# A mixture of experts and two hybrid layers on one core: the last two expert turns written out, the expert output spread in two parts by token tile, the first layer's norm between its adds

## The reference, cut to what matters

```python
out = jnp.zeros_like(t)
for e in range(N_EXPERTS):                       # 32 experts, D_FF_EXP = 512
    hid = jax.nn.silu(t @ w_eg[e]) * (t @ w_eu[e])
    out = out + gates[:, e:e + 1] * (hid @ w_ed[e])
...
x = x + hier_moe(h2, w_rg[l], b_rg[l], w_re[l], b_re[l], w_eg[l], w_eu[l], w_ed[l])
...                                              # first_block ends in rmsnorm(x, normf_g)
h = rms_norm(x, norm_mix)                        # hybrid_layer, DEPTH_2 = 2 times
proj = h @ w_in
```

## Time and profile before

| | |
|---|---|
| median of 3 runs | 1846.59 us |
| profiled execution | 1845.76 us |
| its span | 1844.0 us |
| PE busy | 1741.5 us, 94% of the span |
| DVE, ACT, POOL busy | 883.2, 730.7, 109.2 us |
| moved | 412.19 MB |
| experts on PE (first `pick` to last `spread`) | 181.7 to 651.7 us |

### The profile page before, as it was taken

The page is one execution under the profiler, slowest core; times in us unless marked ns, Lnnn a source line. Parts: engine busy times, 40 slices in busy tenths (PEclk is TensorE's granted clock), DMA queues, the critical chain, the costliest instruction groups (busy, mean ns, idle before and its releaser), DMA issues.

```text
span 1844.0 us, 27291 instructions
## 1 busy us (share of the span) xinstructions
PE 1741.5 (94%) x11548; PEld 1384.4 (75%) x11548; DVE 883.2 (48%) x1445; ACT 730.7 (40%) x1076; POOL 109.2 (6%) x116
## 2 busy tenths in 40 slices
PE   7996999889998889999999999999999999999998
PEld 6985344434444379888899999888988889989986
DVE  5484111111111164643468966536553447886643
ACT  4462111111111044654556444324575455644432
POOL 0000000000000001410200000000150020000000
PEclk9997999999999988999999999999999999999999
DMA  7344799999999845233334354544433233444452
GB/s 270 119 186 188 303 429 429 428 430 428 428 429 428 364 184 228 93 138 138 124 122 160 144 190 183 207 159 180 187 138 134 95 137 138 164 185 162 183 212 98
DMA packets 31304, 412.19 MB, mean 224 GB/s; under 512 B 3649, under 2 KB 5217, under 8 KB 6497
## 3 DMA queue, kind: packets, MB, share of 16 engines
q1 hardware_dynamic: 31200, 410.70, 55.9%
HBM read 408.85 MB, written 1.84 MB: 223 GB/s over the span
## 4 chain that ended last, share of the span: by engine, by line
PE 83%; DMA 9%; DVE 3%; ACT 2%; issue 2%; SPq 0%; POOL 0%; DVEq 0%; POOLq 0%; ACTq 0%
PE bank L1149 11%; PE bank L1154 11%; PE bank L1150 11%; PE bank L1064 9%; DMA work_mem<-in_w 8%; PE bank L1162 4%; PE bank L1163 4%; PE bank L1161 4%; PE bank L1081 4%; PE bank L1187 2%; PE bank L1188 2%; PE bank L1193 2%; DMA wring<-in_w 1%; PE bank L1473 1%; PE bank L1043 1%
## 5 line engine op out<-in xcount | busy, mean ns | idle before, releaser
L1789 ACT ACTIVATE w_hi<-wring 128x2048 fp32r<-128x2048 f32 x84 | 161.0, 1917 | 252.1 <-PE bank L1150 130.8
L2473 DVE TENSOR_TENSOR w_lo<-wring,w_hi 128x2048 fp32r<-128x2048 f32 x84 | 192.1, 2291 | 136.0 <-ACT w_hi L1789 135.9
L1149 PE MATMUL bank<-mixed_hi,w_hi_early 128*128 128x256 f32 x960 | 241.5, 290 | 4.9 <-DVE mixed_lo L2481 2.5
L1789 ACT ACTIVATE w_hi_early<-wring 128x2048 fp32r<-128x2048 f32 x84 | 160.7, 1913 | 203.6 <-PE bank L1150 142.6
L1150 PE MATMUL bank<-mixed_lo,w_hi_early 128*128 128x256 f32 x960 | 235.4, 283 | 0.0
L2473 DVE TENSOR_TENSOR w_lo<-wring,w_hi_early 128x2048 fp32r<-128x2048 f32 x84 | 191.6, 2285 | 75.0 <-ACT w_hi_early L1789 74.6
L1154 PE MATMUL bank<-mixed_hi,w_lo 128*128 128x256 f32 x1472 | 206.5, 283 | 0.0
L1149 PEld LDWEIGHTS bank<-mixed_hi,w_hi_early 128*128 128x128 f32 x960 | 183.7, 191 | 11.7 <-DVE w_lo L2473 4.6
L1154 PEld LDWEIGHTS bank<-mixed_hi,w_lo 128*128 128x128 f32 x1472 | 189.9, 192 | 0.0
L1150 PEld LDWEIGHTS bank<-mixed_lo,w_hi_early 128*128 128x128 f32 x960 | 184.3, 192 | 0.1
L1064 PE MATMUL bank<-wring,gates_mem 128*64 128x512 f32 x768 | 168.3, 594 | 12.3 <-DMA wring<-in_w 12.3
(11 more groups left out here) (482 smaller groups left out, 3089.0 us busy)
## 6 DMA issues: line engine op xcount, KB each, us to landing
wring<-in_w SPq DMA_DIRECT2D x160, 2048.0 KB, 8.8
work_mem<-in_w SPq DMA_DIRECT2D x32, 2048.0 KB, 17.9
cst<-in_const SPq DMA_DIRECT2D x1, 1224.0 KB, 16.3
prm<-in_prm SPq DMA_DIRECT2D x3, 381.0 KB, 8.6
x_mem<-in_x SPq DMA_DIRECT2D x2, 512.0 KB, 4.9
out_x<-x_mem SPq DMA_DIRECT2D x2, 512.0 KB, 2.6
rel_skew<-work_mem SPq DMA_DIRECT2D x1, 768.0 KB, 3.5
work_mem<-in_prm SPq DMA_DIRECT2D x1, 512.0 KB, 16.4
```

Of the source, the lines that this page charges most:

```text
L1149: pe.matmul(out, w[0][:, k, cols], x[0][:, k, :], start=(k == 0), stop=False)
L1789: act.activation(hi, w, ACT.Copy).then_inc(hi_ready, 1)
L2473: dve.tensor_tensor(lo, w, hi, ALU.subtract).then_inc(lo_ready, 1)
```

## The change

The table of steps has `flip 1` ahead of `down`, a `down` of two jobs and a `spread` of four; `plan_layer` gives `nsa_k` three banks in place of two.

```diff
-             ("down_a", 0), ("flip", 1), ("down_b", 0), ("down_a", 1), ("down_b", 1),
-             ("spread_a", 0), ("spread_b", 0)]
-MOE_JOBS = {"pick": 4, "spread_a": 2, "spread_b": 2}
+             ("flip", 1), ("down", 0), ("down", 1), ("spread", 0)]
+MOE_JOBS = {"pick": 4, "down": 2, "spread": 4}
```

On TensorE the steps are written as functions that take the pair, `down` and `spread` in parts, and called in a new order:

```diff
+            def down(pair, e):
+                half = slice(e * CAP, (e + 1) * CAP)
+                if e == 0:
+                    copied(r["flip", pair][0])
+                w = weight("down", pair, e)
+                for n, j in enumerate(r["down", pair]):
+                    if e == 0:
+                        ready(j)
+                    for ft in range(4):
+                        mm = pe.matmul(psum[j.bank][half, :], hid_t[:, pair, ft, half], w[:, ft, n * 512:(n + 1) * 512],
+                                       start=(ft == 0), stop=(ft == 3))
+                    if e == 1:
+                        mm.then_inc(r.bank_full[j.bank], 1)
+            def spread(pair):
+                copied(r["turn", pair][0])
+                for n, j in enumerate(r["spread", 0]):
+                    i, half = divmod(n, 2)
+                    copied(r["down", pair][half])
...
+                    pe.matmul(psum[j.bank][:, :], w, ye_hi[:, pair, cols], start=(pair == 0), stop=False)
+                    mm = pe.matmul(psum[j.bank][:, :], w, ye_lo[:, pair, cols], start=False, stop=(pair == PAIRS - 1))
...
+            hidden("up", 1)
+            down(0, 0)
+            flip(1)
+            down(0, 1)
+            down(1, 0)
+            spread(0)
+            down(1, 1)
+            spread(1)
-        with pe.Fori(0, MOE_TURNS) as turn:
+        with pe.Fori(0, MOE_TURNS - 2) as turn:
             experts(first_pass, turn, turn, 0)
         pe.wait_ge(crowded_ready, 1)
         with pe.If(pe.value_load(crowded[0:1, :], min_val=0, max_val=1) > 0):
...
+        with pe.Else():
+            for turn in range(MOE_TURNS - 2, MOE_TURNS):
+                experts(first_pass, turn, turn, 0)
```

SyncE issues the layers' first three chunks as soon as `up 1` and `down 0` of the last turn have filled their banks, where it waited for all of the last turn:

```diff
+                if l == 0 and c < RING:
+                    j = moe[chunk_users[turn_chunks - MOE_SLOTS + c]][-1]
+                    sp.wait_ge(bank_full[j.bank], j.count(last_turn))
```

```diff
+            add_spread(first_pass, 0, last_turn)
+            add_spread(first_pass, 1, last_turn)
+            gain_x(0)
+            add_spread(first_pass, 2, last_turn)
+            add_spread(first_pass, 3, last_turn)
...
+        eps_in(0)
         var_in(0, 0)
+        gain_x(1)
         diag_in(0, 0)
+        eps_in(1)
         var_in(0, 1)
         diag_in(0, 1)
...
-            split_lo(0)
             dve.wait_ge(params2_loaded, 16 * l + 16)
             low_x(layer["ht"], at2["norm_mix"], h_lo, 0)
+            split_lo(0)
```

`split_hi(0)` of the second layer stands at the end of the first layer on ScalarE, and `split_hi(1)` ahead of `high_x` there. The layer's first product runs the high passes of both tiles, each in a bank of its own, and then the low ones:

```diff
+            def split_first(jobs):
+                pe.wait_ge(hi_ready, PRE_HALVES + HALVES * l + 1)
+                for t, j in enumerate(jobs):
...
+                        pe.matmul(out, w[:, k, :], h_hi[:, k, :], start=(k == 0), stop=False)
+                        pe.matmul(out, w[:, k, :], h_lo[:, k, :], start=False, stop=False)
+                half_ready(0)
+                for t, j in enumerate(jobs):
+                    for k in range(KT):
+                        mm = pe.matmul(psum[j.bank][:, 0:S], lo[:, k, t * P:(t + 1) * P], h_hi[:, k, :], start=False,
+                                       stop=(k == KT - 1))
```

More of the change, by code:

```diff
@@ new lines, in weight, with pick @@
+            def weight(name, pair, e):
+                c = MOE_CHUNKS.index((name, pair, e))
+                pe.wait_ge(r.w_landed[c % MOE_SLOTS], moe_landed(c, at))
+                return moe_slot(c).rearrange("p (k n) -> p k n", k=4 if name == "down" else KT)
+            def pick():
+                pe.wait_ge(r.slots_ready, slots_before + turn + 1)
+                for n, j in enumerate(r["pick", 0]):
+                    ready(j)
+                    for k in range(2):
+                        cols = slice((2 * n + k) * P, (2 * n + k + 1) * P)
+                        for i in range(TT):
+                            pe.matmul(psum[j.bank][:, k * S:(k + 1) * S], xn_hi[:, i, cols], one_hot[:, i],
+                                      start=(i == 0), stop=False)
+                            mm = pe.matmul(psum[j.bank][:, k * S:(k + 1) * S], xn_lo[:, i, cols], one_hot[:, i],
+                                           start=False, stop=(i == TT - 1))
+                    mm.then_inc(r.bank_full[j.bank], 1)
@@ new lines, in turn_hot @@
+            def turn_hot(pair):
+                j, two = r["turn", pair][0], slice(2 * pair, 2 * pair + 2)
+                out = psum[j.bank]
+                ready(j)
+                for i in range(TT):
+                    pe.transpose(out[:, i * P:(i + 1) * P], one_hot_f[:, i, two, :], ident)
+                for i in range(TT):
+                    mm = pe.matmul(out[:, S:S + 1], weighted[:, i, two, :], C("one"), start=(i == 0), stop=(i == TT - 1))
+                mm.then_inc(r.bank_full[j.bank], 1)
@@ new lines, in hidden @@
+            def hidden(name, pair):
+                j = r[name, pair][0]
+                ready(j)
+                w = [weight(name, pair, e) for e in range(2)]
+                for k in range(KT):
+                    if name == "gate" and pair == 0 and k % 2 == 0:
+                        copied(r["pick", 0][k // 2])
+                    for e in range(2):
+                        half = slice(e * CAP, (e + 1) * CAP)
+                        mm = pe.matmul(psum[j.bank][half, :], x_e[:, k, pair, half], w[e][:, k, :], start=(k == 0),
+                                       stop=(k == KT - 1))
+                mm.then_inc(r.bank_full[j.bank], 1)
@@ L2385, in slots, with add_spread, experts @@
             dve.tensor_tensor(weighted, one_hot, now[1], ALU.mult).then_inc(r.slots_ready, 1)
-        def experts(r, turn, at, made):
-            downs = [s for s in MOE_STEPS if s[0] in ("down_a", "down_b")]
+        def add_spread(r, n, at):
+            j, (i, half) = r["spread", 0][n], divmod(n, 2)
+            xs = x[:, i, half * 512:(half + 1) * 512]
+            dve.wait_ge(r.bank_full[j.bank], j.count(at))
+            dve.tensor_tensor(xs, psum[j.bank][:, :], xs, ALU.add).then_inc(r.bank_read[j.bank], 1)
+        def experts(r, turn, at, made, last=False):
             for step, pair in MOE_STEPS:
                 if step in ("pick", "turn", "flip"):
+                    continue
+                if step == "spread":
+                    for n in range(0 if last else 4):
+                        add_spread(r, n, at)
                     continue
```

214 lines of the change are left out of this document (97 added, 117 removed).

## The result

The changed kernel takes 1906.05 us (median of 4 runs, 1905.28 to 1906.56) against 1846.24 us (4 runs, 1841.85 to 1846.78): a ratio of 1.0329, with an interval of 1.0311 to 1.0347. It is 3.3% slower, 59.8 us, and 8 us less slow than forecast. The profiled execution took 1905.64 us, 59.9 us more than that of before. The page of the profile after: span, TensorE's busy time, and what was moved in 40 slices.

A forecast was written before the change was run, and what follows sets the result against it. Transfers bound the experts' turns; TensorE would become the bound at 67.1 us a turn. Experts +69.9 us, tail -3.3, layer 0 +1.7, layer 1 -0.9: +67.4 us, giving 1914 us, range 1897 to 1935.

The forecast's parts named there:

- Two halves run side by side only when neighbours are in different halves: TensorE's `down`: 64-column matmuls of one expert, all in one half of the array, cannot overlap; each row costs 0.43 us.
- The three rivals: Hidden and faster, 1841 us, chance 0.05; weights late as well, 1938 us, 0.08; half clock in one-sided stretches, 2130 us, 0.03.
- +13.3 us of `down` in a turn: Each turn's `down` goes from 32 pairs of rows, 13.75 us, to 64 rows, 27.5 us, less 0.43 at one border.
- the 0.3 us for the column mode: In each turn, one more change from 64 to 128 columns and back on TensorE, 0.3 us.
- 1.1 us for the last `spread`: In each turn, the second `spread` directly behind `down(1,1)` stalls for the last `ye_hi` and `ye_lo`, 1.1 us.
- The branch at 1.5 us, 0 to 4: TensorE's flag and branch between the sixth and seventh turn, with no slack behind it, cost 1.5 us.
- The first turn +2: The first turn's `pick` starts at half clock, which slack hid before; up to 3.8 us more, taken as +2.
- Tail: From the last `down` through the norm to the first product: 4.0 us less, of which -3.3 us is counted.
- T + 14.8: Start of the first product, counted from T, the end of the last `down`; before the change T + 18.8.
- Layer 0, +1.7 us for `split_lo(1)`: In layer 0 the second job's low weights come 6.0 us behind `low_x`, TensorE wants them at 4.4: +1.7 us.
- Layer 1, −0.9: In layer 1 `split_lo(0)` no longer holds up `low_x`: -1.1 us, of which -0.9 is kept.
- Layers' chunks earlier: 0: The layers' first weight chunks come during the last turn, but nothing on the path waited for them: 0 us.

The follow-up runs named there:

- the two built on it: That best version with `spread` filling its banks in order 0, 2, 1, 3: 1842.51 us; then also `spread(0)` ahead of the second pair's `down`: 1842.25 us.

## Why the prediction came out as it did

The forecast was 1914 us with 1897 to 1935; 1906.05 lies in it. The cause it named is shown from both sides: put into the kernel before, the order in `down` costs 44.5 us; taken out of the changed kernel it gives back 52.8. The two differ because the turns do, 63.9 us and 65.3: the kernel with the order alone has a `down` of 24.5 us and not 26.2, and no wait of 0.9 us for `ye_lo`, but waits 1.8 us for weights. The number is better than its parts: a term 14 us too high and one 6.5 us too low were added. Point by point:

- *Two halves run side by side only when neighbours are in different halves.* Right: 7.03 us for 16 rows (6.9 forecast), single weight loads 0.43 us apart. The three rivals fell with it: no turn of 59 us, no granted clock of 0.5 in `down` (1.00 over the third turn), and no wait for weights, so that `up 1` comes in time.
- *+13.3 us of `down` in a turn.* Mis-sized, +12.0: the pieces are 7.03, 12.2 and 7.0 us against 14.2 before (I took 13.75 by the pace in place of the rows' own 3.65, 3.5 and 7.09). The border between the halves saves three rows and not one, 1.5 us and not 0.43. With the 0.3 us for the column mode, which did not show, and 0.9 in place of 1.1 us for the last `spread`, the turn is 65.3 us where 67.1 was forecast: 8 x 1.8 = 14 us too many.
- *The branch at 1.5 us, 0 to 4.* Wrong, 8.0 us: 5.9 us idle, and 2.1 us because the clock had fallen to half in the idle time and `pick` ran at it. The step that failed took VectorE's 0.74 us and SyncE's 1.3 us for TensorE. The profile before did hold it: TensorE stood still from 651.7 to 659.80, all put down to VectorE's diagonal, with a 5.78 us branch inside that ended 0.45 us before. I read the 8.13 us as a wait for data alone. The two errors, 14 us too many and 6.5 too few, have opposite signs; that they leave 8 us of 59.8 is luck.
- *The first turn +2.* Right, 2.4 over the other turns, where TensorE is the bound.
- *Tail.* T + 14.8 forecast, T + 14.3 measured (712.4 to 726.65). The timeline of VectorE shows the chain as it was described: adds of token tile 0, its gain, adds of tile 1, two diagonals.

```profile
714.58 1.29 DVE L2458 TENSOR_TENSOR x_mem<-bank,x_mem 128x512 f32<-128x512 f32 x2 [0.50 <-issue]
715.90 1.22 DVE L2500 TENSOR_TENSOR work_mem<-x_mem,work_mem 128x1024 f32<-128x1024 f32 x1
717.04 1.28 DVE L2458 TENSOR_TENSOR x_mem<-bank,x_mem 128x512 f32<-128x512 f32 x2
...
720.20 0.28 DVE L2544 TENSOR_SCALAR work_mem<-cst,small 128x128 f32<-128x128 f32 x1 [0.44 <-POOL small L2096]
```

- *Layer 0, +1.7 us for `split_lo(1)`.* Right at its place, +1.4, but not in the total, since by the next layer's norm nothing of it is left. TensorE's timeline has it at the second job's start, which came 6.66 us behind the first product before and comes 8.11 us behind it now:

```profile
726.65 0.36 PE L1199 MATMUL bank<-mixed_hi,w_hi_early 128*128 128x256 f32 x1 [0.66 <-DVE mixed_lo L2570]
...
734.76 0.38 PE L1180 MATMUL bank<-mixed_hi,w_hi_early 128*128 128x256 f32 x1 [1.28 <-DVE w_lo L2562]
```

- *Layer 1, −0.9.* Right: TensorE's wait for `mixed_lo` there is 0.7 us, and was 1.8.
- *Layers' chunks earlier: 0.* Right as a price, and no gain either. But in the kernel before they were in flight during the branch, which was 2.4 us longer for it, all beside the norm.

The range stated for the forecast's own case, 1902 to 1924, is also mis-added above: 8, 2.5 and 2 us on 1914 are 1926.5.

What stays open: the first turn, which is 60.2 to 61.7 us in six of the seven profiles that have the new code and alternate in the first turn, with 58.5 in the seventh, against 58.7 and 59.0 in two with the old code; no run isolates why. The timelines show where 1.6 of the 2 us lie: behind the last chunk of that turn the kernel with the branch at the end needs 12.3 us to the next `pick` and the kernel before 10.8, with `spread(0)` between the two jobs of `down` and 0.9 us for `ye_lo`. The seventh profile is the one with `spread(0)` ahead of them (9.7 us), but two of its later turns take 60.4 and 60.1 us and one 55.7. Open too is the start of the experts, 182.0 to 184.4 us in the ten profiles built on the changed kernel, 179.5 to 182.3 in the three on the other. And the 3.9 us between the medians 1846.68 and 1842.74 have no cause in the traces. Small differences are hard to assign here: from the first product to the end the thirteen profiles take 1174.4 to 1177.9 us, with almost the same code. The best version that the experiments point to, alternating `down`, branch at the end and `split_lo(0)` first in layer 0, takes 1842.74 us (the two built on it are not to be told from it), 0.2% below the kernel before, less than the 0.3% of the prediction's text, though its interval over 11 runs excludes 1.

## What to carry to other kernels

Matmuls of 64 columns are cheap only by their neighbour: alternate the halves matmul by matmul, and never order a product by expert because its weights come by expert. Before TensorE work is added to a turn that the transfers bound, count the slack (here 6.4 us) and price the addition against that. And place a branch of TensorE's over a large body where another engine's chain makes it wait anyway and no large transfer runs; look for its record inside idle times that the profile gives to other causes.

## What the runs showed of the hardware that I had not expected

- TensorE's trace has rows of the other half that start ahead of three rows which come earlier in the program (296.62 before 297.04), and hardly more: with blocks of eight rows of each half in turn, 16 rows take 5.39 us, not 3.65.
- The branch over the flag's body takes TensorE 3.38 to 3.86 us in seven traces with few or no weights in flight (4 to 106 GB/s), and 5.78 to 7.62 us in six with the queue at over 400 GB/s. The same instruction takes it 0.08 to 0.24 us at the end of a turn's loop, and the other engines 0.04 to 0.07 us.
- In the idle time behind the sixth turn the granted clock fell to 0.50, half of 2.4 GHz (581 to 583), and `pick` ran at 0.50 for its first 4 us: an idle time of 5.9 us cost 8.0.
